# Reordering the work between the levels of a recurrent core: a bonus sum, three key rows and a group norm change their places

## What is computed

```python
    kk = heads(k * k_k)
    kk = kk / jnp.maximum(jnp.sqrt(jnp.sum(kk * kk, axis=-1, keepdims=True)), 1e-12)
    k = k * (1.0 + (a - 1.0) * k_a)
    y = rwkv7_scan(rh, heads(decay), kh, vh, -kk, kk * ah)
    mean = jnp.mean(y, axis=-1, keepdims=True)
    var = jnp.mean(jnp.square(y - mean), axis=-1, keepdims=True)
    yn = ((y - mean) * lax.rsqrt(var + RW_GN_EPS)).reshape(B, T, D)
    yn = yn * ln_w.astype(f32) + ln_b.astype(f32)
    bonus = jnp.sum(rh * kh * r_k.astype(f32), axis=-1, keepdims=True) * vh
    out = (yn + bonus.reshape(B, T, D)).astype(x.dtype) * g
```

## Time and profile before

| what | us |
|---|---|
| median of 3 runs | 3548.57 |
| lowest, highest | 3538.01, 3551.53 |
| profiled execution, its own time | 3546.89 |
| span of the profile, first to last instruction | 3545.1 |
| TensorE's granted clock, mean over the span | 0.98 |

### The profile page before, as it was taken

How to read it: one execution, slowest core, us unless ns; L and a number is a source line. 1 busy time by engine, 2 the same in 40 slices (tenths; PEclk the granted TensorE clock), 3 DMA queues, 4 the chain that set the end, 5 groups by cost and what they waited for, 6 DMA issues and landing times. The chain is left out here.

```text
span 3545.1 us, 61068 instructions
## 1 busy us (share of the span) xinstructions
PE 3413.6 (96%) x25036; PEld 2755.3 (78%) x25036; DVE 1991.8 (56%) x2398; ACT 1194.3 (34%) x1597; POOL 1590.6 (45%) x1148
## 2 busy tenths in 40 slices
PE   8998999999999999999999899999999999999989
PEld 6886778888888777788787777888888887674767
DVE  7885555556224642226767647555642458768452
ACT  4553233332112362225555524333310231232221
POOL 3442377774333333333444325777633323560352
PEclk9998999999999999999999999999999999999999
DMA  2110122224311142231212211222332113111312
GB/s 103 48 56 30 37 83 87 78 83 154 107 47 55 48 173 90 99 144 38 86 45 86 68 36 54 89 83 83 109 135 79 60 35 121 60 48 42 101 43 76
DMA packets 74064, 274.58 MB, mean 77 GB/s; under 512 B 8209, under 2 KB 8593, under 8 KB 73361
## 3 DMA queue, kind: packets, MB, share of 16 engines
q1 hardware_dynamic: 68112, 250.79, 21.0%
q10 hardware_dynamic: 5760, 20.97, 1.5%
HBM read 207.77 MB, written 63.96 MB: 77 GB/s over the span
## 5 line engine op out<-in xcount | busy, mean ns | idle before, releaser
L121 POOL TENSOR_TENSOR gap<-ones 128x1 f32<-128x1 f32 x150 | 45.6, 304 | 1236.2 <-PE ps L171 780.9
L124 POOL TENSOR_TENSOR wlo<-wraw,whi 128x1024 fp32r<-128x1024 f32 (+3 forms) x150 | 391.6, 2610 | 12.5
L916 DVE TENSOR_TENSOR h<-ps,h 128x1024 f32<-128x1024 f32 (+1 forms) x56 | 68.5, 1223 | 286.1 <-PE ps L420 256.9
L171 PE MATMUL ps<-xh,whi 128*128 128x512 f32 x640 | 203.7, 400 | 22.2 <-ACT rw_stage L1911 5.4
L171 PE MATMUL ps<-xl,whi 128*128 128x512 f32 x640 | 199.6, 394 | 0.0
L171 PE MATMUL ps<-xh,wlo 128*128 128x512 f32 x640 | 198.9, 392 | 0.0
L1030 POOL TENSOR_TENSOR wlo<-wraw,whi 128x512 fp32r<-128x512 f32 x126 | 167.1, 1341 | 50.6 <-ACT whi L1153 50.4
L122 POOL TENSOR_SCALAR whi<-wraw 128x1024 fp32r<-128x1024 f32 (+3 forms) x150 | 179.8, 1199 | 0.2 <-issue 0.2
L388 ACT ACTIVATE sq<-h 128x1024 f32<-128x1024 f32 x32 | 34.0, 1061 | 394.2 <-DVE h L916 304.0
L2223 POOL TENSOR_TENSOR rw_levels<-rw_levels,rw_masks 128x512 f32<-128x512 f32 x64 | 87.3, 1379 | 176.7 <-PE ps L2312 141.1
L171 PEld LDWEIGHTS ps<-xh,whi 128*128 128x128 f32 x640 | 119.8, 190 | 56.5 <-issue 8.2
(11 more groups left out here) (673 smaller groups left out, 9559.3 us busy)
## 6 DMA issues: line engine op xcount, KB each, us to landing
wraw<-w_ffn_in SPq DMA_DIRECT2D x88, 512.0 KB, 3.5
ffn_hidden<-sum_of_squares SPq DMA_DIRECT2D x44, 512.0 KB, 2.6
rw_next<-rw_kept SPq DMA_DIRECT2D x40, 512.0 KB, 5.1
wraw<-w_ffn_out SPq DMA_DIRECT2D x32, 512.0 KB, 3.6
ffn_stage<-ffn_hidden SPq DMA_DIRECT2D x30, 512.0 KB, 4.6
rw_kept<-rw_stage SPq DMA_DIRECT2D x24, 512.0 KB, 2.7
rw_kept<-rw_stage ACTq DMA_DIRECT2D x24, 512.0 KB, 2.7
wraw<-w_ple SPq DMA_DIRECT2D x16, 640.0 KB, 3.9
```

What stands on the lines that cost most here:

```text
L121: nc.gpsimd.tensor_tensor(g.gap[:, 0:1], g.ones[:, 0:1], g.ones[:, 0:1], ALU.mult)
L124: nc.gpsimd.tensor_tensor(g.wlo[:, s, 0:w], g.wraw[:, s, 0:w], g.whi[:, s, 0:w].bitcast(F32), ALU.subtract).then_inc(g.w_split.sem, 1)
L171: last = nc.tensor.matmul(acc[:, hf, :], w[:, s, c:c + P], x[:, kt, hf * HALF:(hf + 1) * HALF], start=start and kt == 0 and n == 0, stop=s ...
L916: nc.vector.tensor_tensor(ht, flat(banks(g, acc + 2 * s)), ht, ALU.add).then_inc(g.acc_free.sem, 1)
```

## The change

On PE the next pair's bonus sum goes from behind the solutions to between the last corrections and the last inverses. On ACT `blend` goes from behind level 3's copies to directly behind `log_key`, `inverse_deviation` from the end of the last level to behind level 3's copies, and `decay_until` ahead of both copies of the last level. On VectorE `key_rate`, the row `kt` (now `scaled_key`, split from `scaled`) and `receiver_key` go between the growing of level 1 and of level 2; `unit_rate`, `group_norm` and `group_bias` go ahead of `whole`. On POOL `gated` goes ahead of `hats`. No operation is added or removed.

```diff
@@ gpsimd, for m
+            if m:
+                gated(m - 1)
             if m + 1 < KD:
                 hats(m + 1)
-            if m:
-                gated(m - 1)
@@ tensor, for m
             for h in (0, 1):
                 last_corrections(m, h)
+            if following:
+                bonus_sum(m + 1)
             for h in (0, 1):
                 last_inverses(m, h)
             if prior:
                 pe.wait_ge(g.y_ready.sem, g.y_ready.base + m)
             solutions(m)
-            if following:
-                bonus_sum(m + 1)
             outputs(m, prior, following)
@@ scalar, for m
             if following:
                 log_key(m + 1)
+                blend(m + 1)
             else:
                 high(2)
...
             keep_correction(m, 3, 0)
             keep_correction(m, 3, 1)
+            if prior:
+                inverse_deviation(m - 1)
             if following:
-                blend(m + 1)
+                decay_until(m + 1)
             else:
                 high(4)
             keep_correction(m, LAST, 0)
-            if following:
-                decay_until(m + 1)
-            else:
+            keep_correction(m, LAST, 1)
+            if not following:
                 high(5)
-            keep_correction(m, LAST, 1)
-            if prior:
-                inverse_deviation(m - 1)
@@ vector
+        def scaled_key(m):
+            dve.wait_ge(g.key_ready.sem, g.key_ready.base + m + 1)
+            nc.vector.tensor_tensor(kt, kx, e2, ALU.mult)
+
         def scaled(m):
 
             dve.wait_ge(g.exp_ready.sem, g.exp_ready.base + m + 1)
             nc.vector.scalar_tensor_tensor(at, kk, -1.0, sw, ALU.mult, ALU.mult)
-            nc.vector.tensor_tensor(bt, a, e2, ALU.mult)
-            nc.vector.tensor_tensor(kt, kx, e2, ALU.mult).then_inc(g.hat_go.sem, 1)
+            nc.vector.tensor_tensor(bt, a, e2, ALU.mult).then_inc(g.hat_go.sem, 1)
...
             grow(m, 1, 0)
             grow(m, 1, 1)
+            if following:
+                key_rate(m + 1)
+                scaled_key(m + 1)
+                receiver_key(m + 1)
             grow(m, 2, 0)
             grow(m, 2, 1)
...
             grow(m, 3, 0)
             grow(m, 3, 1)
             if following:
-                key_rate(m + 1)
+                unit_rate(m + 1)
             else:
                 low(1)
+            if prior:
+                group_norm(m - 1)
+                group_bias(m - 1)
             whole(m, 0)
             whole(m, 1)
-            if prior:
-                group_norm(m - 1)
             if following:
-                receiver_key(m + 1)
-                unit_rate(m + 1)
                 scaled(m + 1)
-            if prior:
-                group_bias(m - 1)
-            if following:
                 bonus_read(m + 1)
```

More of the change, by code:

```diff
@@ L2758, in _ @@
         bonus_read(0)
+        scaled_key(0)
         scaled(0)
```

## The result

The changed kernel takes 3600.82 us (median of 6 runs, 3594.53 to 3613.78); the kernel before took 3550.72 in its 6 runs. The ratio on record is 1.0152, with an interval of 1.0136 to 1.0169 (the quotient of these two medians is 1.0141): slower by about 1.5%. The forecast was 3582.6, slower. As a time, the measured median lies 1.2 us inside the upper end of the range, 3602; as a ratio, 1.0152 lies just above it (3602 / 3548.57 = 1.0151). So the direction held, and the size fell short by 18 us. The profiled execution took 3601.21 with a span of 3599.4, which is 54.3 more than the span of before; the forecast sum was 34.0.

The account below looks back on a forecast made before the run. PE's chain was taken as the bound. Four low-clock pairs at 5.9, two full-clock at 2.3, pair 0's 4.5 and pair 7's 1.3 make 34.0; on 3546.89 that is 3580.9, plus 1.7 for the median: 3582.6 us, range 3555 to 3602.

Parts of the forecast that it names:

- Blend: ACT, behind log_key: blend delays level 2's copies, so PE's inverses start 1.0 us later, inside the key rows' term.
- Key rows in the slot: VectorE before level 2's growing: three key rows alternate with POOL's masks, so grow (2,0) starts 3.5 us later.
- the lower bound: VectorE's key rows without exclusion by POOL: grow (2,0) starts only 1.4 us later.
- Level 3 at the lower clock: PE, level 3: new idle lowers the clock, +2.7 us a pair, taken for four of six pairs.
- The tail: First last correction to first output matmul: -1.2 us at full clock, -0.3 if low until the bonus sum lifts it.
- Pair 0: First pair: no norm, one POOL operation more in the queue, small tail gain; +4.5 us.
- Pair 7: Last pair, no following pair: norm and bias come before whole, half in waiting time; +1.3 us.
- POOL, and receiver: POOL's gated before hats makes nothing wait; VectorE's receiver falls from 2.16 to 1.2 under PE's cover; worth 0.
- the clock stays high: Rival, PE in level 3: the clock does not fall there; 3568 us, chance 0.17.
- the key rows fit nearly: Rival, VectorE's slot: no exclusion, or VectorE keeps its turn; 0.2 us in each of six pairs, 3553 us, chance 0.13.
- Faster: Rival, start of next pair: hats and receiver come sooner, so its steps start earlier; -2.8 us a pair, 3533 us, chance 0.07.
- Table loads: Rival, ACT: blend between two logarithms causes two table loads a pair; 9 us in all, 3592 us, chance 0.04.

Follow-up runs that it names:

- e1: Kernel before, with only blend moved on ACT to directly behind the key's logarithm: 3571.14 us, ratio 1.0063.
- e3: Changed kernel, with POOL masking only one of eight tiles in level 3 and making the chunk rates later: 3587.55 us, ratio 1.0113.
- e4: Changed kernel, with ACT's growth directly behind decay and blend ahead of log_key: 3576.8 us, ratio 1.0085.
- e6: Changed kernel, with dense matmuls nobody reads (fillers) added around level 2's inverses and between the last corrections: 3586.21 us, ratio 1.0094.
- e7: Kernel before, with two fillers (dense matmuls nobody reads), one between the last corrections and one behind them: 3547.74 us, ratio 0.9994.
- e8: e4 with the bias behind whole, one filler between level 2's inverses and one between the last corrections: 3563.73 us, ratio 1.0041.
- e9: e7 with more fillers, ahead of pair 7's second inverses of level 1 and ahead of the steps ending the core: 3539.25 us, ratio 0.9983.

## Why the prediction was right in direction and too small

Forecast 34.0, measured 54.3. By its own steps:

- **Blend.** Forecast 1.0 of idle ahead of the inverses; it is 0.80, in e1 and in the changed kernel. Right, a little high.
- **Key rows in the slot.** Forecast +3.5 for grow (2,0) against the logarithm of the key; measured (1939.81 - 1931.97) - (1898.75 - 1894.34) = 3.43, and level 2 +3.40. The order of alternation came out as written, and e3 shows that it is exclusion: without it +1.43 is left, as the lower bound had it. Right.
- **Level 3 at the lower clock.** Forecast +2.7, measured +2.79. The size was right and the count was not: I took four of six pairs, and it was all six and pair 0 too. That is 2 pairs of six, some 6 us of the 20 missing, and part of pair 0's. The reason given, idle ahead of these levels, is what e1 and e4 show.
- **The tail.** Forecast -0.3 at the low clock and -1.2 at the full one, measured +1.51: this is the step that failed. It assumed that the bonus sum would lift the clock while it ran (2.75, last inverses 1.25). The sum ran at 0.50 from end to end or nearly so, 3.72 to 3.78, and the inverses behind it took 1.2 to 1.9, so the solutions started at 7.0 to 7.6 and not at about 6.0. In pairs 3 and 5 part of the solutions was slow as well (6.3 to 6.5 from their start to the outputs, against 4.82 in the others). Where the clock held, in e6, the tail was 10.34 for a forecast of 10.05: the working at full clock was right, but its condition was not met once. Nor was the -1.2 the moved sum's: it set a tail at full clock against 11.24, a tail in which the clock falls. With the clock held, the old order takes 9.39 (e7) and the new one 9.94 (e8) to 10.34 (e6), so at the same clock the new order's tail is the longer one. Six pairs make 9.1 where the forecast had 4 x -0.3 + 2 x -1.2 = -3.6: 12.7 of the missing 20.
- **Pair 0.** Forecast +4.5, measured +9.3. The one more POOL operation is there (level 2 +5.1 for 4.6), but neither level 3's +2.7 nor a dearer tail was in the sum.
- **Pair 7.** Forecast +1.3, its tail measured +1.1; not forecast were 1.6 less in its level 1.
- **POOL, and receiver.** Forecast worth 0. The stage *next* is 21.84 for 21.91, though `receiver` fell from 2.16 to 1.22:

```profile
1969.03 1.22 DVE L2665 TENSOR_TENSOR rw_now<-rw_next 128x1024 f32<-128x1024 f32 x1
```

Of the rivals, *the clock stays high* and *the key rows fit nearly* fell, the latter by e3. *Faster* fell as well: its place was the start of the next pair, and that stage is within 0.2 of before in every kernel that moved the key rows, but for e6, where it is longer. *Table loads* fell by ACT's rows above. The rule of TensorE: Matmul & The Clock Gate (the Trainium skill, "A second HAM failure mode"), that short idles between groups are enough to swing the clock, would have had every pair pay. The trace of the changed kernel agrees, with seven of seven; that of e1, with the 0.80 alone, agrees in five of pairs 1 to 6 and not in pair 4.

Open is how much idle is needed for the clock to fall. Among the pairs 1 to 6, 0.80 sufficed in five of e1 and in one it did not; 0.53 sufficed in all six of e4.

## What to carry to other kernels

A slot in one engine's queue is only as wide as what its work excludes on another engine and as what comes before it in a third: here 4.1 us idle on VectorE held 2.15 of real time, and POOL took two of the three rows' time again. Where a chain consists of thin matmuls, price a new idle not by its length but by the clock that it may cost the stages behind it: 0.8 us idle cost 2.8 here, and a sum of four wide matmuls (by the profile's count) did not bring the clock back in time. Compare a new order with the old one at the same clock: the gain forecast for the tail was the clock's and not the order's. Before reordering, test the clock with a few dense fillers at the waits. In this kernel fillers alone gained 8 us (e9), more than any order tried, and two of them per tail without those of pair 7 gained nothing (e7).

## What the runs showed of the hardware that was not expected

Two fillers, each counted as two 128x128x256 matmuls of 0.70 together, one between and one behind the last corrections, held the clock at 1.00 through the tail in pairs 0 to 6 (e7); in pair 7 it had fallen before, within the first stretch of 27.31. Six fillers in the idle stretches of e6, and one in the tail, held it through level 3 and the tail in two pairs of six. The stretches of 27.31 at 0.50 in e7 had PE busy for 26.88 and 27.31 of it; e3 has one of 30.7. Why the clock doesn't rise there was not found. With the fillers of e9 these stretches are gone, which shows only that they depend on what comes before.
